# Layer 0 of a two-layer decoder step: index products in units 3 and 4, top-k rounds and page loads moved, V pages on halves of x

## What is computed

```python
s = jnp.einsum('bqhe,bse->bqhs', qi, idx_keys)                       # 8 index heads
score = jnp.einsum('bqhs,bqh->bqs', jax.nn.relu(s), wi) * IDX_SCALE
score = jnp.where(admissible[None], score, NEG)
_, idx = lax.top_k(score, topk)
logits = jnp.einsum('bqgrd,bqkgd->bqgrk', qg, k_sel) * ATTN_SCALE    # 16 heads, 4 KV heads
logits = jnp.where(valid, logits + bias, NEG)
out = jnp.einsum('bqgrk,bqkgd->bqgrd', softmax(logits), v_sel)
```

## Time and profile before

| | |
|---|---|
| three runs | 1251.89, 1253.24, 1255.35 us (median 1253.24) |
| the profiled execution | 1253.29 us; span from first to last instruction 1251.6 us |
| PE busy | 1200.9 us (96%), 9582 instructions |
| DVE busy | 708.9 us (57%), 1456 instructions |
| ACT busy | 475.0 us (38%), 872 instructions |
| POOL busy | 82.2 us (7%), 118 instructions |
| mean granted TensorE clock | 0.991 |
| mean DMA rate | 105 GB/s |

### The profile page before, as it was taken

One profiled execution on the slowest core, in us unless ns is written; L12 is line 12 of the kernel. 1 busy time (PEld: TensorE's weight loads), 2 busy tenths in 40 slices (PEclk: granted clock), 3 DMA queues, 4 the chain that ended last, 5 costly groups with the idle time before them and its releaser, 6 DMA issues.

```text
span 1251.6 us, 25585 instructions
## 1 busy us (share of the span) xinstructions
PE 1200.9 (96%) x9582; PEld 1105.5 (88%) x9582; DVE 708.9 (57%) x1456; ACT 475.0 (38%) x872; POOL 82.2 (7%) x118
## 2 busy tenths in 40 slices
PE   8999979999999999999999999899999999999995
PEld 4958735589899999999999988698999999999994
DVE  2288989857943342443447866778533433433477
ACT  2342127744531331332334566634422322312332
POOL 4334300100012000000000000000000000000000
PEclk9999989999999999999999999999999999999998
DMA  6698472043222222232223221141222322222222
GB/s 204 184 277 264 132 245 67 2 153 118 68 68 101 84 89 96 84 101 84 100 85 118 67 74 43 45 147 38 72 97 84 101 85 96 89 84 100 84 85 69
DMA packets 61958, 131.00 MB, mean 105 GB/s; under 512 B 7819, under 2 KB 34603, under 8 KB 61755
## 3 DMA queue, kind: packets, MB, share of 16 engines
q1 hardware_dynamic: 47899, 115.16, 28.3%
q10 hardware_dynamic: 10624, 8.26, 2.2%
q0 software_dynamic: 3360, 6.56, 1.7%
HBM read 125.41 MB, written 9.79 MB: 108 GB/s over the span
## 4 chain that ended last, share of the span: by engine, by line
PE 73%; DVE 12%; issue 6%; POOLq 3%; ACT 2%; POOL 2%; SPq 1%; DMA 1%; DVEq 0%; ACTq 0%
PE PS L605 56%; PE PS L635 7%; PE PS L1020 3%; PE PS L780 2%; PE PS L793 2%; PE PS L807 2%; DVE YA L1640 2%; SPq L395 1%; DVE YA L1627 1%; POOLq L386 1%; DVE RSTD L1632 1%; POOL IK L408 1%; POOLq L406 1%; DMA KVX<-cacheV 1%; DVE X L1646 1%
## 5 line engine op out<-in xcount | busy, mean ns | idle before, releaser
L1483 DVE TENSOR_TENSOR WLO<-WRAW,WHI 128x1024 fp32r<-128x1024 f32 x118 | 145.3, 1231 | 321.3 <-ACT WHI L1082 321.3
L1082 ACT ACTIVATE WHI<-WRAW 128x1024 fp32r<-128x1024 f32 x126 | 133.4, 1059 | 387.9 <-PE PS L605 358.9
L605 PE MATMUL PS<-XH,WHI 128*128 128x260 f32 x1184 | 241.3, 285 | 0.9 <-DVE XL L1808 0.7
L605 PE MATMUL PS<-XH,WLO 128*128 128x260 f32 x1184 | 239.2, 284 | 0.0
L605 PE MATMUL PS<-XL,WHI 128*128 128x260 f32 x1184 | 238.7, 283 | 0.0
L605 PE MATMUL PS<-HH,WHI 128*128 128x260 f32 x944 | 191.2, 284 | 0.2 <-DVE HL L1507 0.2
L605 PE MATMUL PS<-HH,WLO 128*128 128x260 f32 x944 | 190.2, 283 | 0.0
L605 PE MATMUL PS<-HL,WHI 128*128 128x260 f32 x944 | 189.9, 283 | 0.0
L605 PEld LDWEIGHTS PS<-XH,WHI 128*128 128x128 f32 x1184 | 182.8, 189 | 6.4 <-issue 5.4
L605 PEld LDWEIGHTS PS<-XH,WLO 128*128 128x128 f32 x1184 | 183.2, 189 | 0.0
L605 PEld LDWEIGHTS PS<-XL,WHI 128*128 128x128 f32 x1184 | 182.6, 189 | 0.0
(11 more groups left out here) (293 smaller groups left out, 1857.6 us busy)
## 6 DMA issues: line engine op xcount, KB each, us to landing
WRAW<-wall SPq DMA_DIRECT2D x168, 512.0 KB, 3.3
bias_skewed<-bias_seq SPq DMA_DIRECT2D x4, 1280.0 KB, 18.8
X<-xT SPq DMA_DIRECT2D x4, 520.0 KB, 6.7
X<-xT SPq DMA_DIRECT2D x1, 2080.0 KB, 11.6
yT<-X SPq DMA_DIRECT2D x8, 260.0 KB
KVB<-cacheK SPq DMA_DIRECT2D x16, 128.0 KB, 3.0
KVX<-cacheK SPq DMA_DIRECT2D x16, 128.0 KB, 2.6
KVB<-cacheK POOLq DMA_DIRECT2D x16, 128.0 KB, 7.0
```

Source lines behind the costliest of these rows:

```text
L605: mm = pe.matmul(PS[:, 2 * slot + g, 0:TG], w[:, slot, k, :], x[:, k, TG * g:TG * g + TG], start=(k == 0 and w is WHI and x is hi), stop=( ...
L1082: nc.scalar.activation(WHI[:, slot], WRAW[:, slot], ACT.Copy).then_inc(hi_done, 1)
L1483: V.tensor_tensor(WLO[:, slot], WRAW[:, slot], WHI[:, slot].bitcast(F32), ALU.subtract).then_inc(lo_dve, 1)
```

## The change

- Index products go to units 3 and 4, twelve in each, three ahead of every second k step, in the order of head pairs (h, h+1) for t = 1, 2, 3. `sample_scores` and `sample_sums` move to k steps 2 and 4 of unit 5. ScalarE copies KIT in its unit 1; VectorE's low parts of units 4 to 7 move to fit, and the query copies follow the last index sum.
- `SLOT_OF` becomes (1, 2, 3, 4, 6, 7, 8, 9, 11, 12, 13): the search starts half a unit after the samples' sums and ends half a unit sooner.
- Top-k rounds are dealt out anew: 18 half rounds ahead of the search (20 before), one a digit and two at digit 4 (two each before), one a step of the search (4, 2, 2 before), 10 and 12 around the query copies (10 and 14), 2 during the exponential (as before), 10 in `sample_a(-1)` (16), two each in steps 0 to 3 and three each in 4 to 11 (one each in 2 to 11 before).
- The loops over pages of GpSimd, and SP's loop over units 10 to 15, are written out. SP's reads of page numbers, all ahead of unit 9's load before, go behind the loads of units 10 to 13, two samples each; ScalarE's stay at its unit 6, whose eviction of the samples' scores moves to unit 5.
- KVR becomes four tiles, each on a half of XH or XL. V pages of samples 8 and 10 (`V_HALF`), on the halves with k = 0 to 3, are issued when TensorE is through k step 3 of unit 13 (`x_used`).
- ScalarE copies PNEW before PTD; TensorE's new-key products wait for the first alone. The t = 0 part of BT is copied from BT0 by ScalarE, ahead of the exponential, and the transfer of the t = 1 part, now 1 MB for 2 MB, moves behind PTD.

```diff
-V_LATE = (8, 9, 10, 11, 13, 14, 15)
+V_HALF, V_LATE = (8, 10), (9, 11, 13, 14, 15)
-SLOT_OF = (2, 3, 4, 5, 6, 7, 8, 9, 12, 13, 14)
+SLOT_OF = (1, 2, 3, 4, 6, 7, 8, 9, 11, 12, 13)
-        KVR = place("KVR", [P, 4, NPG, 256], at=xw)
+        KVR = [place(f"KVR{n}", [P, NPG, 256], at=xw + n * KT // 2 * TOK) for n in range(4)]
+        def load_first_values(eng, q, numbers):
+
+            eng.wait_ge(x_used, 1)
+            for n in V_HALF:
+                load_sample(eng, q, n, numbers)
...
@@ SP
-            numbers = page_numbers(sp, 0, (12,) + V_LATE)
             early(POOL_LO[0] // 2, 1)
...
-            with sp.Fori(POOL_LO[0] // 2 + 1, POOL_LO[1] // 2) as i:
-                for s in range(2):
-                    sp.wait_ge(lo_pool, i * 2 + (s - 1 - POOL_LO[0]))
-                    load_unit(i * 2 + s, s)
+            late = (12,) + V_HALF + V_LATE
+            numbers = {}
+            for u in range(POOL_LO[0] + 2, POOL_LO[1]):
+                sp.wait_ge(lo_pool, u - 1 - POOL_LO[0])
+                load_unit(u, u % 2)
+                some = late[2 * (u - POOL_LO[0] - 2):][:2]
+                numbers.update(page_numbers(sp, 0, some))
             sp.wait_ge(mask_done, 1)
             load_sample(sp, 0, 12, numbers)
+            load_first_values(sp, 0, numbers)
             load_values(sp, 0, numbers)
@@ GpSimd
-                with pool.Fori(0, 4 - half * IDX_SP) as c:
+                for c in range(4 - half * IDX_SP):
                     for pg in range(NPG):
                         load_index_page(pool, half, c, pg, idx_in)
...
             for n in (6, 7):
-                with pool.Fori(0, NPG) as pg:
+                for pg in range(NPG):
                     load_page(pool, n, pg)
...
+            load_first_values(pool, 1, numbers)
             load_values(pool, 1, numbers)
@@ TensorE
+                    if u == A_OUT - 1 and k == KT // 2 - 1:
+                        mm.then_inc(x_used, 1)
...
-            items = [(t, h) for t in range(1, QT) for h in range(IDXH)]
+            items = [(t, h + e) for h in range(0, IDXH, 2) for t in range(1, QT) for e in range(2)]
...
+                    if t == 1 and h % 2 == 0:
+                        pe.wait_ge(ev_act, h // 2 + 1)
...
-                if u == 5:
-                    between = {k: (lambda k=k: index_scores(3 * k, 3 * k + 3))
-                               for k in range(KT)}
-                elif u == 6:
-                    between = {2: sample_sums}
+                if u in (3, 4):
+                    n = 12 * (u - 3)
+                    between = {k: (lambda n=n + 3 * k // 2: index_scores(n, n + 3))
+                               for k in range(0, KT, 2)}
+                elif u == 5:
+                    between = {2: sample_scores, 4: sample_sums}
...
+                pe.wait_ge(dt_ev, 2)
                 for quad in (range(0, 4), range(4, 8)):
@@ ScalarE
                 if u == 6:
-                    numbers = page_numbers(act, 2, V_LATE)
+                    numbers = page_numbers(act, 2, V_HALF + V_LATE)
+                if u == 5:
...
+                if u == A_OUT - 1:
+                    load_first_values(act, 2, numbers)
...
-                if u == 2:
+                if u == 1:
                     act.wait_ge(kit_mm, 1)
...
+            act.wait_ge(kv_used, DB)
+            act.wait_ge(toe_in[0], 16)
+            nc.scalar.activation(BT[:, :, 384:512], BT0[:], ACT.Copy).then_inc(bt_copy, 1)
             act.wait_ge(d_mx, 1)
...
+            act.wait_ge(dt_mm, 1)
+            nc.scalar.activation(PNEW[:], PS[0:DB, 6, 0:P], ACT.Copy).then_inc(dt_ev, 1)
+            nc.scalar.activation(PTD[:].rearrange("p k r -> p (k r)"), PSF[:, 2048:2048 + 1024],
+                                 ACT.Copy).then_inc(dt_ev, 1)
             act.wait_ge(toe_skew, 16 * 4)
-            act.wait_ge(kv_used, DB)
             load_bias(1)
@@ VectorE
-            for u in range(2, 6):
+            for u in range(2, 4):
                 low_part(u, u % 2)
...
-                if n == 8:
-                    low_part(6, 0)
-                if n == 16:
-                    sample_queries()
+                if n == 4:
+                    low_part(4, 0)
+                if n == 13:
+                    low_part(5, 1)
...
+            sample_queries()
...
-            prompt_rounds(10)
-            low_part(7, 1)
+            low_part(6, 0)
+            prompt_rounds(9)
             dve.wait_ge(ds_ev, 1)
...
-                prompt_rounds(1)
+                prompt_halves(2 if r == 4 else 1)
+                if r == 0:
+                    low_part(7, 1)
...
-                prompt_rounds(1 if i else 2)
+                prompt_halves(1)
...
-            prompt_rounds(7)
+            prompt_rounds(6)
...
                 if i == -1:
-                    prompt_rounds(8)
-                elif i >= 2:
-                    prompt_halves(1)
+                    prompt_rounds(5)
+                else:
+                    prompt_halves(3 if i >= 4 else 2)
```

More of the change, by code:

```diff
@@ L355, in program @@
         qb_ready = sem("qb_ready")
+        x_used, bt_copy = sem("x_used"), sem("bt_copy")
         kv_used = sem("kv_used")
@@ L378, in kv_place @@
             pl = KV_PLACE[n]
-            return (KVB[:, pl] if pl < 4 else KVR[:, pl - 4] if pl < 7 else
+            return (KVB[:, pl] if pl < 4 else KVR[pl - 4][:] if pl < 7 else
                     KVI[:, pl - 7] if pl < 9 else KVX[:, pl - 9] if pl < 11 else
-                    (KVW[:, 0], KVR[:, 3], KVZ[:], KVW[:, 1])[pl - 11])
+                    (KVW[:, 0], KVR[3][:], KVZ[:], KVW[:, 1])[pl - 11])
         def page_number(eng, n, pg):
@@ L572, in _ @@
             for n in (6, 7):
-                with pool.Fori(0, NPG) as pg:
+                for pg in range(NPG):
                     load_page(pool, n, pg)
-            numbers = page_numbers(pool, 1, V_LATE)
+            numbers = page_numbers(pool, 1, V_HALF + V_LATE)
             pool.wait_ge(ds_mm, 3)
             nc.gpsimd.memset(QB[:], 0.0).then_inc(z_qb, 1)
-            with pool.Fori(0, 4) as pg:
+            for pg in range(4):
                 load_page(pool, 3, pg)
@@ L896, in _ @@
                     pe.transpose(PS[0:HD, 6, 0:DB], WD[:], CST[0:DB, 0:DB]).then_inc(kit_mm, 1)
-                if u == 5:
+                if u == 3:
                     pe.wait_ge(kit_ev, 2)
                     pe.wait_ge(wb_ev, 1)
-                    pe.wait_ge(ev_act, 4)
-                if u == 6:
-                    sample_scores()
                 wait_lo(u)
@@ L1040, in sample_b @@
                 if i == 13:
-                    pe.wait_ge(dt_ev, 2)
+                    pe.wait_ge(dt_ev, 3)
                     pe.wait_ge(vwin_in, 16 * DB)
@@ L1316, in _ @@
             nc.scalar.activation(KSD[:], KMV[:, :, 1], ACT.Sqrt, bias=EPSC[:]).then_inc(ksd, 1)
-            items = [(t, h) for t in range(1, QT) for h in range(IDXH)]
+            items = [(t, h + e) for h in range(0, IDXH, 2) for t in range(1, QT) for e in range(2)]
             for u in range(STATIC_UNITS):
-                if u == 5:
-                    for n, (t, h) in enumerate(items):
+                if u in (3, 4):
+                    for n in range(12 * (u - 3), 12 * (u - 3) + 12):
+                        t, h = items[n]
                         act.wait_ge(is_mm, n + 1)
@@ L1374, in load_bias @@
             def load_bias(t):
-                c0, c1 = 384 - P * t, 512 if t == 1 else 512 - P * t
+                c0, c1 = 384 - P * t, 512 - P * t
                 act.dma_start(BT[:, :, c0:c1], bskew[:, :, 127 + c0:127 + c1]
                               ).then_inc(toe_in[t], 16)
+            act.wait_ge(kv_used, DB)
+            act.wait_ge(toe_in[0], 16)
+            nc.scalar.activation(BT[:, :, 384:512], BT0[:], ACT.Copy).then_inc(bt_copy, 1)
             act.wait_ge(d_mx, 1)
@@ L1381, in _ @@
                                  accum_out=DST[:, 2:3]).then_inc(d_exp, 1)
+            act.wait_ge(dt_mm, 1)
+            nc.scalar.activation(PNEW[:], PS[0:DB, 6, 0:P], ACT.Copy).then_inc(dt_ev, 1)
+            nc.scalar.activation(PTD[:].rearrange("p k r -> p (k r)"), PSF[:, 2048:2048 + 1024],
+                                 ACT.Copy).then_inc(dt_ev, 1)
             act.wait_ge(toe_skew, 16 * 4)
-            act.wait_ge(kv_used, DB)
             load_bias(1)
-            act.wait_ge(dt_mm, 1)
-            nc.scalar.activation(PTD[:].rearrange("p k r -> p (k r)"), PSF[:, 2048:2048 + 1024],
-                                 ACT.Copy)
-            nc.scalar.activation(PNEW[:], PS[0:DB, 6, 0:P], ACT.Copy).then_inc(dt_ev, 1)
             def sample_a(i):
@@ L1770, in softmax_in @@
                         dve.wait_ge(toe_in[t], 16)
+                        if t == 1:
+                            dve.wait_ge(bt_copy, 1)
                     for j, (e, g, at) in enumerate(tn.heads_at(i)):
@@ L1906, in _ @@
                 wi = NAT[:, t, HD + h:HD + h + 1]
+                if n:
```

(4 more changed lines are left out.)

## The result

The changed kernel takes 1265.73 us (median of 4 runs, 1263.81 to 1266.58) against 1253.1 for the kernel before: ratio 1.0092, interval 1.0077 to 1.0108, 12.6 us slower where 3.2 faster was forecast. The time lies above the stated range, and it came by another mechanism than that of the slower rival C. The profiled execution took 1266.58 us, its span is 1264.6. VectorE has the instructions that it had (1456); what differs is where they and TensorE stand still.

The account below looks back on a forecast made before the run. Bound changes by stage: TensorE to 98.9, then TensorE with waits, VectorE in the first half of the prompt's attention loop. 0.95 + 5.3 + 12.3 - 15.4 = 3.15 us off 1253.24 gives 1250.1; range 1244 to 1256.5.

Parts of the forecast that it names:

- rival C: Steps 2 to 11 of the prompt's attention: TensorE at half clock loses 1.5 us a step, up to 1262; chance 0.13.
- Index products: Units 3 to 6: 24 products in 11.84 against 12.15, no last-ReLU wait of 0.75, unit 6 ending at 98.0, 0.95 earlier.
- GpSimd: Written-out page loops: 1.13 us a page, 12.6 us saved, GpSimd free at 92 to 94 for unit 8's low part.
- Rival B: Written-out GpSimd pages are no quicker, unit 8's low part again ends near 107.9: 1255.2 us; chance 0.09.
- Unit 8: TensorE's 2.51 us wait for the low part and 1.65 of half clock go; collision 0.95, unit 10's 1.0.
- SP's 32 reads ... Nothing: SP's page-number reads moved behind weight loads, 4.3 us a unit, cost nothing; uncovered 4.3 once.
- V pages: Samples' attention: 7.34 MB at 347 GB/s takes 21.1 us, in by 161.5; margin 2 us, lateness 0 to 3.
- Half rounds: Steps 0 to 11: 22 more top-k half rounds at 0.758 us, 16.6, less 1.2: stretch grows 15.4 us.
- Rival A: VectorE's added half rounds and collisions fall partly into waits, saving 3 and 1.6 us more: 1245.5; chance 0.20.
- D: Arrival at softmax_in(2) 3 us later than laid, no cover for added rounds: 1253, no change; chance 0.16.
- The change touches no line there: From 266.6 us on, MLP and layer 1, 985.0 of 1251.6 us: no line changed.

Follow-up runs that it names:

- x1: The changed kernel with SP's four bias transfers moved ahead of unit 8's weight load: 1257.29 us, ratio to before 1.0032.
- x5: The changed kernel with V pages of samples 8 and 10 issued behind k step 6 of unit 13 instead of 3: 1267.64 us.
- x9: x8 with the first quad's V pages shared 3, 3, 2 among SP, GpSimd and ScalarE instead of 4, 2, 2: 1252.64 us, ratio 0.9988.
- x2: The changed kernel with eight top-k half rounds moved from steps 4 to 11 into VectorE's wait ahead of softmax_in(2): 1260.17 us.
- x8: x1 with ten half rounds moved from steps 0 to 11 into digit 4, the search's first step and the wait ahead of softmax_in(2): 1251.55 us.
- b2: The kernel before with six half rounds moved from steps 2 to 7 into the wait ahead of softmax_in(2): 1254.46 us, ratio 1.0002.
- x1 to x5: Five variants of the changed kernel; those not listed singly: GpSimd's page loops restored, 1264.66 us; first quad's V pages shared 2, 3, 3, 1266.85 us.
- x10: x1 with ScalarE's 14 page-number reads moved ahead of its work on the samples' scores in unit 5: 1257.24 us.
- x12: x8 with one half round in the search's first step, eight in digit 4, and x10's edit: 1249.15 us, ratio to before 0.9965.

## Why the prediction was wrong

Of the 16.5 us between 1250.1 and the profiled 1266.58:

- **Start, 1.3.** The first index product came at 53.01; in the profile of before unit 3 begins at 51.72. This is a difference between executions, not a term of the change.
- **Index products: right.** From a group of three to the next work it is 1.27 or 1.69 us, 11.87 in all (laid 11.84); there is no wait for the last ReLU; unit 6 ends at 99.54, which is 98.0, the later start and 0.2.
- **GpSimd: right.** A page is 0.54 + 0.62 = 1.16 (laid 1.13), and GpSimd is free from 92.6. Rival B fails. The two cache lines that the Trainium skill gives such an engine (Advanced Engine Details and Errata, ISA Cache) show no price here: a page written out takes 1.16 us for 1.27 and 1.5 in the loops, and the page of the profile has 28 packets for 26 in the instruction queue q14.
- **Unit 8: right.** WHI was ready at 102.67 and the low part at 105.14, laid at 100.8 and 103.2; the later start comes to both, and some 0.6 more. The collision laid at 0.95 is 1.14, the other laid at 1.0 is 1.13; VectorE's operation on two SBUF inputs stood 1.97 us from 103.19, until 105.15, beside the low part from 102.75 to 105.14. The Trainium skill (SBUF — State Buffer, SBUF: two separate sides) has one of two such operations fully blocked until the other, which started first, is through, and the trace agrees.
- **"SP's 32 reads ... Nothing": the step that failed, 6.3.** I followed SP's issue of unit 9's weights (94.5 laid, 96.25 measured) and took the landing for granted. The price was in the flight: 18.0 us behind 5.2 MB of bias transfers that the change had pushed 11.3 us later without touching them. The prediction has no term for them. Unit 9 waits 4.65, then runs its first half in 4.75 us instead of 3.07 at the lower clock, 1.7 more. x1 shows the cause, and all ten profiles of the changed kernel and its variants have the load landing right behind these transfers. What the prediction missed is the path: the step moved was TensorE's, and the transfers hung on it by unit 4, high part 6, low part 6 and unit 8's load.
- **V pages: a term mis-sized, 4.4.** I laid all seven samples' 7.34 MB at 347 GB/s, in by 161.5, 22.1 us behind the first issue, and tested that sum against the second quad alone, with a margin of 2. From the first issue at 148.71 the last V page took 28.1 us, to 176.78. By the rows below (columns as in rows 1) the first 5.3 us ran at 166 and 230 GB/s, not at 347, and in the 28.1 us 8.4 MB moved: the difference is about the t = 1 part of BT, 1.05 MB issued at 166.65, which the sum left out. The two quads' bytes are interleaved, so the first quad, too, gets its last page late, at 170.34. It waited 2.68 and ran 2.8 slower for it at the lower clock, less 1.1 by which TensorE came earlier than laid, counted from unit 13's end. x5 shows that it was bound by data; and the margin for the second quad wasn't there either, as x9 shows with its wait of 3.39.

```profile
148.70:151.40 2.70, 2.70 (x24) 2.56 (x22) 1.91 (x7) 0.00 (x0) 2.07 (x4) 1.00 0.56 166
151.40:154.00 2.60, 2.60 (x15) 1.26 (x18) 1.80 (x6) 2.09 (x3) 1.89 (x5) 1.00 0.90 230
...
148.70:176.80 28.10, 25.06 (x251) 13.58 (x249) 24.18 (x93) 12.46 (x40) 7.53 (x14) 0.88 0.98 299
```

- **Half rounds: right, and they made the loss.** Laid at +15.4, measured 56.4 - 41.3 = 15.1; x2 and x8 price one at 0.72 to 0.73. The trade that I forecast, 18.5 us of earlier arrival at `softmax_in(2)` for 15.4 given back in the steps, became 5.0 for 15.1. VectorE then stood 5.23 us just ahead of the loop while half rounds waited inside it. Rival C fails: the clock of steps 2 to 11 was 1.00. Rival A fails: VectorE was busy 96% of it. D had the right direction, with 3 us for what was 13.6.
- **"The change touches no line there": 2.9, not shown to be the change's.** In layer 1 TensorE waits 1.44 us at one place in both kernels. In the profile of before the clock stayed at 1.00, in that of the changed kernel it fell to 0.50. But it fell in the second profile of the kernel before as well (0.65 over four us), in b2, and in x1 to x5 and x10; it did not in x8 and x9, and in x12 only in part.

6.3 + 4.4 + 1.3 + 2.9 is 14.9; of the remaining 1.6 some 1.1 lie in units 7 to 13, 0.3 of them in the two collisions, and the rest in small differences of the other stages. The medians say the same: 12.6 lost against before, of which x1 gives back 8.4 and the half rounds, once moved, 5.7 to 8.1 (x8 and x12 against x1), together more than the loss.

What stays open: what sets the 9.8 us that unit 9's weights still fly in x1, from 95.17, when the last bias transfer was under way, to 105.00; how much of the first V quad's wait is due to the slow start of the pages and how much to BT, since no run moves BT alone; and why the fall in layer 1 comes in one execution and not in another.

## What to carry to other kernels

When work is moved on one engine, follow the buffers that it frees to the transfers that wait for them, and price those in the place where they now fly, not only where they are issued: a transfer whose own lines didn't change can be what the next load queues behind. When several groups' bytes are interleaved, test data against its first consumer, not its last, and count every transfer that flies with them. Filler such as top-k rounds belongs in measured waits: the same half round is free in one of 3 us and costs its whole 0.73 in a loop that its engine bounds; and where an expected earlier arrival is paid for in advance by filler put behind it, the payment is due even if the arrival fails. A wait that gets shorter doesn't show that the edit did it: look at what the awaited work itself waited for (x10).

## What the runs showed of the hardware

The granted clock after a short wait isn't a property of the program alone. At the same 1.44 us wait of the same instructions in layer 1 it fell to its lower level in nine profiles, for half as long in that of x12, and held in the first of before, in x8 and in x9; in the changed kernel's profile the part behind unit 14 was 2.9 us longer than in the first of before. In the second profile of before it also fell behind a wait of 1.18 us in the index products of unit 5, and stayed at 0.50 from 70 to 80; the samples' scores began at 90.28 instead of 83.56. Falls of this size fit the spread of the kernel before, 1250.1 to 1258.7 over its runs. In all ten profiles with index products in units 3 and 4 there is no wait among them, and no such fall.

The other fact is on one queue. A weight load that SP issued behind the four bias transfers of 1.3 MB landed only after these: asked for at 81.35 (x1) and at 96.25 (the changed kernel), its 512 KB flew 20.8 and 18.0 us, where the median weight load of the changed kernel flew 3.2.
